# One decoder layer on one core: the router finishes its expert weights later, gathers spread over more banks, and the first norm's factor is computed ahead of the parameters

## The chip, the cores and the metric

The kernel is one launch on one core of a Trainium2 chip. The metric is the device time of that launch in microseconds (us), lower is better. The engines are PE (TensorE), DVE (VectorE), ACT (ScalarE), POOL (GpSimd) and SP (SyncE, which here only issues DMAs). They run side by side and meet at semaphores. A bank is one of the eight PSUM banks into which PE writes.

## The reference, cut to what matters

One layer for 256 tokens of width 2048, in float32: a norm and one big projection, two mixers (sparse attention and RWKV-7), an output projection, attention over 256 memory tokens, and then the part that the change is mostly about, a mixture of experts in two levels. A token picks the best of 4 groups, and inside it the best 2 of 8 experts:

```python
def hier_moe(h, wg_r, bg_r, we_r, be_r, w_gate, w_up, w_down):
    hf = h.reshape(B * T, D)
    p_group = jax.nn.softmax((hf @ wg_r + bg_r).astype(jnp.float32), axis=-1)
    pg_top, g_idx = lax.top_k(p_group, 1)
    e_logits = (hf @ we_r + be_r).reshape(n, N_GROUPS, EXPERTS_PER_GROUP)
    e_logits = jnp.take_along_axis(e_logits, g_idx[:, :, None], axis=1)[:, 0]
    p_exp = jax.nn.softmax(e_logits.astype(jnp.float32), axis=-1)
    pe_top, e_idx = lax.top_k(p_exp, TOP_K_INNER)
    wts = pg_top * pe_top / jnp.sum(pe_top, axis=-1, keepdims=True)
    ...
    for grp in range(N_GROUPS):
        sl = slice(grp * EXPERTS_PER_GROUP, (grp + 1) * EXPERTS_PER_GROUP)
        hid = (jax.nn.silu(jnp.einsum("nd,edf->nef", hf, w_gate[sl]))
               * jnp.einsum("nd,edf->nef", hf, w_up[sl]))
        y = y + jnp.einsum("nef,efd->nd", hid * combine[:, sl, None], w_down[sl])
```

The first norm, `h = rmsnorm(x, ln1_g)`, is the other place that the change touches.

## The kernel before, in words

**Precision.** Matmuls that need float32 accuracy are done in three passes: an operand is split into a high part (ACT writes a copy) and a low part (DVE subtracts that copy from the value), and PE multiplies hi by hi, hi by lo and lo by hi.

**Start.** SP loads x and a table of small parameters. ACT sums the squares of x. DVE waits first for PE's transposed parameter table (`prm`, lines 1835 to 1839), copies it, and then computes the norm's factor and two diagonal matrices (`diagonals("n1", D)`, helper lines 1804 to 1817). PE transposes x through these diagonals (line 784), and DVE multiplies each result by the gain (line 1823).

**Router.** PE computes 36 logits per token (line 1195) and turns them (line 1206). DVE then works through a chain of tiny instructions, each waiting for the one before it through a semaphore (`link`): the one-hot of the group `goh`, the logits of the chosen group `d8`, the best and second expert `o1`, `o2` (helper `first_only`, three instructions), their weights `w1_`, `w2_`, and the table `comb` of weights by expert. ACT gives two exponentials on the way, `ge` and `e2`. With the mark `routed` PE counts each token's place in its group (`pos`, lines 1210 to 1212) and the size of each group (`cnt`, line 1215). DVE makes from these the one-hot matrices `G` of two groups of up to 128 tokens each (line 2218) and the flag `oflag` of a group over 128 (line 2223, mark `most`). This input has no such group, so the extra pass over one isn't run.

**Gather.** `gather(k)` on PE first computes each slot's weights from `comb` (line 1228, bank 0, eight matmul records; DVE copies them to `wcol`, line 2241), and then in eight steps f the gathered activations of two groups (line 1238), step f into bank 3 or 2. For each step ACT writes the high part (line 1681) and DVE the low part (line 2246), after which the bank is free. The first gather opens the expert stage, the second comes 15 experts later, at group 2.

**Experts.** An expert is six half units of weights of 2048 columns each: four for gate and up (offsets 0 to 3), two for down (4, 5). SP loads them (line 689, 694), ACT splits off the high part (line 1696), DVE the low part (line 2156), PE multiplies (line 1275 gate and up, line 1294 down). There are three split buffers, so a half unit can be split when PE has read the third one before it. Between gate/up and down stand ACT's tanh (line 1709), DVE's two products `hid` (`hidden_values`, lines 2259 to 2263), and a transpose (line 1283). The kernel runs one expert's gate and up ahead of its down. Between two groups of eight experts PE scatters the sums back to tokens (line 1259), and DVE adds them to x (line 2236).

**Order.** Each engine executes its own list, written out by hand, strictly in order. Before the loop over experts DVE's list is: router chain, low part of half unit 0, gather, low parts of half units 1 to 3, eleven instructions on overflow (`posm`'s and `comb`'s extra column, then the visit count, mark `ovi`), the read of that count into a register, and `hidden_values(0)`.

Of the kernel before, what the change touches and what calls it, by code (L numbers as in the profile page):

```python
# [23 lines left out]
ALU = mybir.AluOpType  # L24
# [49 lines left out]
def decoder_layer(nc, x_in, mem, ln1_g, w_in, cmp_pos_k, cmp_w1_k, cmp_w2_k, cmp_pos_v, cmp_w1_v,  # L74
# [5 lines left out]
    with ctx:  # L80
# [411 lines left out]
        dve_r = Progress(sem("dve_router"), ["h3lo", "gd", "m2", "routed", "posm", "most", "ovi"])  # L492
# [25 lines left out]
        SRC_NA, SRC_N2, SRC_MEM = 1, 5, 13  # L518

# [220 lines left out]
        def _(pe):  # L740
# [468 lines left out]
            pe.wait_ge(*dve_r.at("routed"))  # L1209
# [9 lines left out]

            def gather(k):  # L1220

                pe.wait_ge(onehot_g, k + 1)
                if k:
                    pe.wait_ge(dve_sc, 8 * (2 * k - 1))
                for g in range(2 if k < NGR // 2 else 1):
                    at = (2 * k + g) * EPG
                    for tt in range(NT):
                        mm = pe.matmul(bank[0][:, g * EPG:g * EPG + EPG], G[:, tt, g * P:g * P + P].bitcast(F32),
                                       comb[:, tt, at:at + EPG], start=tt == 0, stop=tt == 1)
                mm.then_inc(pe_cm, 1)  # L1230
                for f in range(8):
                    if f >= 2:
                        pe.wait_ge(dve_hs, 8 * k + f - 1)
                    for j in range(2):
                        c = 2 * f + j
                        for tt in range(NT):
                            for part in range(2):
                                mm = pe.matmul(bank[3 - f % 2][:, j * 2 * P:j * 2 * P + 2 * P],
                                               h3[part][:, tt, c * P:c * P + P],
                                               G[:, tt, :], start=tt + part == 0, stop=tt + part == 2)  # L1240
# [115 lines left out]
        def _(act):  # L1356
# [319 lines left out]
            def gathered(k):  # L1676
                for f in range(8):
                    act.wait_ge(pe_hs, 8 * k + f + 1)
                    for j in range(2):
                        c = 2 * f + j  # L1680
                        ins = A(hs[0][:, :, c, :], b2(3 - f % 2)[:, j, :].rearrange("p (g s) -> p g s", g=2), ACT.Copy,
# [22 lines left out]
            act.wait_ge(*dve_r.at("m2"))  # L1704
            A(e2, m2, ACT.Exp).then_inc(*act_r.mark("e2"))
# [60 lines left out]
            nov = act.value_load(count_i[0:1, 0:1], min_val=0, max_val=1)  # L1766
            tanh(0, 0, 4)
# [29 lines left out]
        def _(dve):  # L1797
# [36 lines left out]

            dve.wait_ge(*pe_c.at("prm"))
# [5 lines left out]
            diagonals("n1", D)  # L1841
# [345 lines left out]
            first_only(o1, eq8, wtie)  # L2187
            link(V.scalar_tensor_tensor(out=flat(d8), in0=flat(o1), scalar=BIG, in1=flat(d8), op0=ALU.mult, op1=ALU.add))
            V.tensor_reduce(m2, d8, AX.X, ALU.max).then_inc(*dve_r.mark("m2"))
            dve.wait_ge(*act_r.at("e2"))  # L2190
            link(TT(eq8, d8, bc(m2.unsqueeze(2), 2, EPG), ALU.is_equal))
            first_only(o2, eq8, wtie)
            link(V.tensor_scalar(w1_, e2, 1.0, None, ALU.add))
            link(V.reciprocal(w1_, w1_))
            link(TT(w1_, w1_, pg, ALU.mult))
            link(TT(w2_, w1_, e2, ALU.mult))
            link(V.tensor_scalar(w1_, w1_, 0.5, None, ALU.mult))
            link(V.tensor_scalar(w2_, w2_, 0.5, None, ALU.mult))
            link(TT(c8, o1, bc(w1_.unsqueeze(2), 2, EPG), ALU.mult))
            link(TT(eq8, o2, bc(w2_.unsqueeze(2), 2, EPG), ALU.mult))  # L2200
            link(TT(c8, c8, eq8, ALU.add))
            link(TT(o1, o1, o2, ALU.add))
            for t in range(NT):
                g4 = bc(goh[:, t].unsqueeze(2), NGR, EPG)
                ins = TT(comb[:, t, 0:NE].rearrange("p (g j) -> p g j", g=NGR), g4, bc(c8[:, t].unsqueeze(1), NGR, EPG),
                         ALU.mult)
            ins.then_inc(*dve_r.mark("routed"))
            dve.wait_ge(*dve_r.at("routed"))
# [7 lines left out]
            for tt in range(NT):  # L2216
# [3 lines left out]


            dve.wait_ge(*pe_r.at("cnt"))
            V.tensor_scalar(oflag, bank[2][:, 128:128 + NGR], float(CAP), None, ALU.is_gt)\
                .then_inc(*dve_r.mark("most"))
            weights(None, 0)
# [12 lines left out]
            def gathered(k):  # L2238
                dve.wait_ge(pe_cm, k + 1)
                w = 2 * EPG if k < NGR // 2 else EPG  # L2240
                V.tensor_copy(wcol[:, 0:w], bank[0][:, 0:w])
                for f in range(8):
                    dve.wait_ge(act_hs, 8 * k + f + 1)
                    for j in range(2):
                        c = 2 * f + j
                        ins = V.scalar_tensor_tensor(out=hs[1][:, :, c, :],
                                                     in0=b2(3 - f % 2)[:, j, :].rearrange("p (g s) -> p g s", g=2),
# [31 lines left out]
            def first_body(n):  # L2279
# [22 lines left out]
                if n:  # L2302
                    add(n - 1, 6)
                    add(n - 1, 7)
                onehots(n, 0)
# [18 lines left out]
            dve.wait_ge(*dve_r.at("most"))  # L2324
            link(TT(geq, pg_, bc(oflag.unsqueeze(1), 2, NGR), ALU.mult))
            link(V.tensor_reduce(rtop, geq, AX.X, ALU.add))
# [186 lines left out]
```

## Time and profile before

| what | us |
|---|---|
| three runs | 1781.06, 1775.94, 1781.58 (median 1781.06) |
| profiled execution, its own time | 1781.15 |
| its span | 1779.4 |
| busy: PE, DVE, ACT, POOL | 1691.9, 1011.4, 760.7, 71.5 |
| mean granted clock of PE | 0.983 of full speed |

The span is what the trace covers, some 1.75 us less than the execution's own time. A busy share near 95% of PE doesn't say that PE bounds every stage. For that the chain of work that ended last is to be read, stage by stage: it names at each moment the instruction that the end was waiting for. Bracketed times in the timeline are idle time of an engine ahead of an instruction, with what released it.

### The profile page before, as it was taken

What the parts mean: (1) busy time and instruction counts of PE and PEld (TensorE: products, weight loads), DVE (VectorE), ACT (ScalarE), POOL (GpSimd) and SP (SyncE); (2) the same over time, 40 slices, a digit from 0 to 9 for tenths busy, and PEclk for the clock granted to TensorE, in tenths of its full rate; (3) what the DMA queues carried; (4) which work ended last, traced back from release to release, by engine and by line L of the source; (5) the groups of instructions that cost most, each with busy time, mean ns of one, the idle gap of its engine ahead of it and who ended that gap; (6) DMA issues with size and microseconds to landing.
All of it is one profiled execution on the core that took longest, in us unless ns stands there. A gap on an engine that the chain in (4) does not pass through costs nothing.

```text
span 1779.4 us, 29542 instructions
## 1 busy us (share of the span) xinstructions
PE 1691.9 (95%) x12488; PEld 1471.4 (83%) x12488; DVE 1011.4 (57%) x1261; ACT 760.7 (43%) x964; POOL 71.5 (4%) x136
## 2 busy tenths in 40 slices
PE   6999999999999999999999999969999999999996
PEld 5887887878878989999999989857887887888784
DVE  1142533424435544445453334468889888889986
ACT  1011210111115444444443334426776766777674
POOL 4001010101100000000000000000000000000000
PEclk9899999999999999999999999989999999999999
DMA  7420613306126434446545235229998996999993
GB/s 209 142 95 3 196 49 127 117 2 196 49 97 211 147 125 136 143 143 198 180 142 189 94 104 187 95 101 358 375 378 329 378 373 239 369 374 361 347 374 153
DMA packets 173745, 350.77 MB, mean 197 GB/s; under 512 B 12915, under 2 KB 145612, under 8 KB 148172
## 3 DMA queue, kind: packets, MB, share of 16 engines
q1 hardware_dynamic: 173644, 349.30, 55.6%
q8 instruction: 78, 1.28, 0.3%
q14 instruction: 23, 0.19, 0.0%
HBM read 347.18 MB, written 2.10 MB: 196 GB/s over the span
## 4 chain that ended last, share of the span: by engine, by line
PE 86%; DVE 10%; ACT 2%; POOL 1%; issue 1%; SPq 0%; DMA 0%; DVEq 0%; ACTq 0%
PE bank L1275 18%; PE bank L765 16%; PE bank L1127 10%; PE bank L1294 9%; PE bank L1131 5%; PE bank L1023 4%; PE bank L1030 4%; DVE split L2156 2%; PE bank L784 2%; PE bank L754 2%; PE bank L870 1%; DVE piece L1977 1%; PE bank L885 1%; PE bank L880 1%; DVE arena_phases L2236 1%; PE bank L1177 1%
## 5 line engine op out<-in xcount | busy, mean ns | idle before, releaser
L2156 DVE TENSOR_TENSOR split<-weights_raw,split 128x2048 fp32r<-128x2048 f32 x192 | 438.6, 2290 | 55.9 <-ACT split L1696 53.2
L1696 ACT CAST split<-weights_raw 128x2048 fp32r<-128x2048 f32 x192 | 367.1, 1913 | 94.0 <-PE bank L1275 48.0
L1275 PE MATMUL bank<-split,gathered_hi 128*128 128x512 f32 x1024 | 321.3, 395 | 7.4 <-DVE split L2156 7.4
L765 PE MATMUL bank<-arena_fixed 128*128 128x256 f32 x1280 | 302.1, 388 | 0.0
L765 PEld LDWEIGHTS bank<-arena_fixed 128*128 128x128 f32 x1280 | 238.1, 191 | 42.7 <-issue 9.1
L1275 PEld LDWEIGHTS bank<-split,gathered_hi 128*128 128x128 f32 x1024 | 190.9, 189 | 48.3 <-DVE split L2156 9.6
L1275 PE MATMUL bank<-split,gathered_lo 128*128 128x512 f32 x512 | 201.0, 393 | 0.0
L1127 PE MATMUL bank<-loop_split,act_over_concat 128*128 128x256 f32 x768 | 164.8, 283 | 0.0
L1294 PE MATMUL bank<-split,hidden_hi 128*128 128x512 f32 x512 | 161.0, 395 | 1.5 <-DVE hidden_lo L2268 1.0
L2060 DVE TENSOR_TENSOR loop_split<-arena_fixed,loop_split 128x2048 fp32r<-128x2048 f32 x48 | 107.8, 2288 | 90.7 <-ACT loop_split L1593 90.7
L1127 PEld LDWEIGHTS bank<-loop_split,act_over_concat 128*128 128x128 f32 x768 | 129.1, 192 | 0.1
L1127 PE MATMUL bank<-loop_split,act_over_hT 128*128 128x256 f32 x512 | 119.0, 283 | 0.0
L1294 PEld LDWEIGHTS bank<-split,hidden_hi 128*128 128x128 f32 x512 | 95.8, 187 | 25.3 <-issue 1.2
L1275 PEld LDWEIGHTS bank<-split,gathered_lo 128*128 128x128 f32 x512 | 96.8, 189 | 21.0
L1294 PE MATMUL bank<-split,hidden_lo 128*128 128x512 f32 x256 | 100.9, 394 | 0.0
L1977 DVE TENSOR_TENSOR piece<-arena_fixed,piece 128x1024 fp32r<-128x1024 f32 x60 | 72.5, 1220 | 41.4 <-ACT piece L1429 41.2
L1131 PE MATMUL bank<-act_over_concat,loop_split 128*128 128x256 f32 x512 | 92.3, 283 | 0.0
L1593 ACT CAST loop_split<-arena_fixed 128x2048 fp32r<-128x2048 f32 x48 | 89.2, 1917 | 5.1 <-PE bank L1023 3.1
L1127 PEld LDWEIGHTS bank<-loop_split,act_over_hT 128*128 128x128 f32 x512 | 89.1, 192 | 0.2 <-DVE loop_split L2060 0.2
L1429 ACT CAST piece<-arena_fixed 128x1024 fp32r<-128x1024 f32 x60 | 62.3, 1044 | 53.2 <-PE bank L1030 25.7
L1131 PEld LDWEIGHTS bank<-act_over_concat,loop_split 128*128 128x128 f32 x512 | 79.9, 192 | 0.0
L1030 PE MATMUL bank<-mem_lo,piece 128*128 128x256 f32 x256 | 73.1, 286 | 0.0
(394 smaller groups left out, 2395.8 us busy)
## 6 DMA issues: line engine op xcount, KB each, us to landing
weights_raw<-in_moe_w_gate_dram SPq DMA_DIRECT2D x64, 1024.0 KB, 4.9
weights_raw<-in_moe_w_up_dram SPq DMA_DIRECT2D x64, 1024.0 KB, 7.0
weights_raw<-in_moe_w_down_dram SPq DMA_DIRECT2D x32, 2048.0 KB, 7.7
arena_fixed<-in_w_in_dram SPq DMA_DIRECT2D x22, 2048.0 KB, 8.8
arena_fixed<-in_wv_mem_dram SPq DMA_DIRECT2D x8, 2048.0 KB, 8.7
arena_fixed<-in_w_out_dram SPq DMA_DIRECT2D x8, 2048.0 KB, 8.2
arena_fixed<-in_wq_mem_dram SPq DMA_DIRECT2D x8, 2048.0 KB, 8.2
arena_fixed<-in_wo_mem_dram SPq DMA_DIRECT2D x8, 2048.0 KB, 8.2
```

The costliest lines, as they stand in the source:

```text
L765: mm = pe.matmul(b[:, half * T:half * T + T], w[:, c, half * P:half * P + P], hT[:, c, :], start=st, stop=en)
L1023: mm = pe.matmul(b[:, half * UC:half * UC + UC], mem_x(x_, c)[:, half * P:half * P + P], pieces[p % NPB][:, w_, at:at + UC], start=False, ...
L1030: mm = pe.matmul(b[:, half * T:half * T + T], pieces[p % NPB][:, w_, at:at + P], mem_x(x_, c), start=c + t == 0, stop=c == NC - 1 and t == 2)
L1127: mm = pe.matmul(b, src(x_, cc)[:, half * P:half * P + P], lspl[2 * s + h][:, y_, c * UC:c * UC + UC], **flags)
L1131: mm = pe.matmul(b, lspl[2 * s + h][:, y_, at:at + P], src(x_, cc), **flags)
L1275: mm = pe.matmul(bank[parity][:, :], hs[a][:, group % 2, NC // 4 * off + c, :], sl[:, b, c * 2 * FF:(c + 1) * 2 * FF], start=off + c + k == 0,
L1294: mm = pe.matmul(bank[4 + q][:, :], tTs[a][:, f, :], sl[:, b, q * 512:q * 512 + 512], start=start and f + k == 0, stop=stop and f + k == 3)
L1593: nc.scalar.copy(lspl[2 * s + h][:, 0, :], slot(s)[:, at:at + HU]).then_inc(loop_hi, 1)
L1696: nc.scalar.copy(split_half(i, 0, j), raw_half(j, hf, tail)).then_inc(act_hi, 1)
L1977: V.tensor_tensor(piece_half(p, 1), raw_piece(p), piece_half(p, 0).bitcast(F32), ALU.subtract) .then_inc(piece_lo, 1)
L2060: V.tensor_tensor(sl[:, 1, :], slot(s)[:, r:r + HU], sl[:, 0, :].bitcast(F32), ALU.subtract)\
L2156: V.tensor_tensor(split_half(i, 1, j), raw_half(j, hf, tail), split_half(i, 0, j).bitcast(F32), ALU.subtract).then_inc(dve_lo, 1)
```

## The change

There are three edits.

1. At the start `diagonals("n1", D)` stands ahead of DVE's wait for the parameter table.
2. The router: DVE forms `goh` first, without the sum and reciprocal of the group softmax, and marks it; PE's `pos` and `cnt` wait for this mark instead of `routed`. DVE goes on to the chosen logits up to `eq8`, then makes positions, `G`, `oflag` and the visit count (`ovi`). The rest of the chain is a function `expert_weights()`, called behind the low parts of half units 1 to 3. One addition (`o1` plus `o2`, whose sum nothing reads) is gone. The slot weights of the first gather are a function of their own, called on PE behind the fourth half unit, into bank 4. The overflow column (`overflow_slots`) is computed in the first expert's body, and DVE reads the visit count after the first group of experts. PE reads it behind the first half unit.
3. The first gather uses banks 3, 2, 4, 5, 6, 7 in turn, later ones 3, 2, 0. The first multiplication after a later gather waits for the sixth low part.

```diff
-            pe.wait_ge(*dve_r.at("routed"))
+            pe.wait_ge(*dve_r.at("goh"))
             pe.matmul(bank[3][:, 0:NGR], strictU, goh[:, 0, :], start=True, stop=True)
...
+        def gather_banks(k):
+            return (3, 2, 0) if k else (3, 2, 4, 5, 6, 7)
...
+            def gather(k):
+                pe.wait_ge(onehot_g, k + 1)
+                banks = gather_banks(k)
+                if k:
+                    pe.wait_ge(dve_sc, 8 * (2 * k - 1))
+                    slot_weights(k, 0)
                 for f in range(8):
-                    if f >= 2:
-                        pe.wait_ge(dve_hs, 8 * k + f - 1)
+                    if f >= len(banks):
+                        pe.wait_ge(dve_hs, 8 * k + f - len(banks) + 1)
+                    elif banks[f] == 0:
+                        pe.wait_ge(dve_hs, 8 * k + 1)
...
-                    pe.wait_ge(dve_hs, 8 * (group // 2) + 2 * off + 2)
+                    pe.wait_ge(dve_hs, 8 * (group // 2) + max(2 * off + 2, 6 if group else 0))
...
             pe.wait_ge(*dve_r.at("most"))
-            pe.wait_ge(*dve_r.at("h3lo"))
             gather(0)
-            for off in range(4):
-                gate_up(None, off, 0, 0, fresh=True)
+            gate_up(None, 0, 0, 0, fresh=True)
             pe.wait_ge(*dve_r.at("ovi"))
             nov = pe.value_load(count_i[0:1, 0:1], min_val=0, max_val=1)
+            for off in range(1, 4):
+                gate_up(None, off, 0, 0, fresh=True)
+            pe.wait_ge(*dve_r.at("routed"))
+            slot_weights(0, 4)
...
+            dve.wait_ge(*pool_c.at("ident"))
+            diagonals("n1", D)
             dve.wait_ge(*pe_c.at("prm"))
             link(V.tensor_copy(prm, bank[2][:, 0:2 * P]))
...
-            diagonals("n1", D)
...
-            dve.wait_ge(*act_r.at("ge"))
-            link(V.tensor_reduce(pg, ge, AX.X, ALU.add))
-            link(V.reciprocal(pg, pg))
+            dve.wait_ge(*dve_r.at("gd"))
             link(V.tensor_scalar(geq, gd_, 0.0, None, ALU.is_equal))
-            first_only(goh, geq, wtie[:, 0:NGR])
+            link(TT(goh, geq, bc(wtie[:, 0:NGR].unsqueeze(1), 2, NGR), ALU.mult))
+            link(V.tensor_reduce(rtop, goh, AX.X, ALU.max))
+            TT(goh, goh, bc(rtop.unsqueeze(2), 2, NGR), ALU.is_equal).then_inc(*dve_r.mark("goh"))
...
-            link(TT(o1, o1, o2, ALU.add))
...
             gathered(0)
             for off in range(1, 4):
                 weights(None, off)
+            expert_weights()
+            slot_weights(0, 4)
             hidden_values(0, 0, 0)
             for n in range(NGR):
                 group(n)
+                if n == 0:
+                    dve.wait_ge(*dve_r.at("ovi"))
+                    nov = dve.value_load(count_i[0:1, 0:1], min_val=0, max_val=1)
```

DVE's list between the group counts and the first split, before. `arena_phases` holds all small router values, `split0` to `split2` the split buffers, `gathered_lo` the low part of the gathered tokens.

```order
L2199 TENSOR_TENSOR arena_phases<-arena_phases 128x16
L2200 TENSOR_TENSOR arena_phases<-arena_phases 128x16
L2201 TENSOR_TENSOR arena_phases<-arena_phases 128x16
L2202 TENSOR_TENSOR arena_phases<-arena_phases 128x16
L2205 TENSOR_TENSOR arena_phases<-arena_phases 128x32 x2
L2211 SCALAR_TENSOR_TENSOR arena_phases<-bank3,arena_phases 128x2x4
L2213 TENSOR_SCALAR arena_phases<-arena_phases 128x2x4
L2214 COPY arena_phases<-arena_phases 128x2
L2218 TENSOR_SCALAR gather_onehots_76<-arena_phases 128x128 x4
L2223 TENSOR_SCALAR arena_phases<-bank2 128x4
L2156 TENSOR_TENSOR split0_64<-weights_raw_67,split0_64 128x2x4x256
L2241 COPY arena_phases<-bank0 128x16
```

And after, at the same place:

```order
L2202 TENSOR_TENSOR arena_phases<-arena_phases 128x16
L2203 TENSOR_SCALAR arena_phases<-arena_phases 128x16
L2207 SCALAR_TENSOR_TENSOR arena_phases<-bank3,arena_phases 128x2x4
L2209 TENSOR_SCALAR arena_phases<-arena_phases 128x2x4
L2210 COPY arena_phases<-arena_phases 128x2
L2214 TENSOR_SCALAR gather_onehots_76<-arena_phases 128x128 x4
L2217 TENSOR_SCALAR arena_phases<-bank2 128x4
L2220 TENSOR_TENSOR arena_phases<-arena_phases 128x4
L2221 TENSOR_REDUCE arena_phases<-arena_phases 128x1
L2222 TENSOR_REDUCE arena_phases<-arena_phases 128x1
L2223 SCALAR_TENSOR_TENSOR arena_phases<-arena_phases 128x1
L2225 TENSOR_SCALAR arena_phases<-arena_phases 128x1
```

The weights' arithmetic no longer stands ahead of the positions (line 2207, which reads bank 3), and the visit count follows line 2217.

DVE's list behind the low part of the fourth half unit, before. `visit_counts` is the table that the engines read into registers.

```order
L2156 TENSOR_TENSOR split0_64<-weights_raw_67,split0_64 128x2x4x256
L2325 TENSOR_TENSOR arena_phases<-arena_phases 128x8
L2326 TENSOR_REDUCE arena_phases<-arena_phases 128x2
...
L2336 TENSOR_SCALAR arena_phases<-arena_phases 128x1
L2337 CAST visit_counts<-arena_phases 128x3
L2339 TENSOR_LOAD visit_counts
L2339 ISA x2
L2259 COPY arena_phases<-arena_phases 128x1
```

And after:

```order
L2172 TENSOR_TENSOR split0_64<-weights_raw_67,split0_64 128x2x4x256
L2183 TENSOR_TENSOR arena_phases<-arena_phases 128x16
L2184 TENSOR_REDUCE arena_phases<-arena_phases 128x2
L2185 TENSOR_TENSOR arena_phases<-arena_phases 128x16
...
L2247 TENSOR_TENSOR arena_phases<-arena_phases 128x16
L2248 TENSOR_TENSOR arena_phases<-arena_phases 128x16
L2251 TENSOR_TENSOR arena_phases<-arena_phases 128x32 x2
L2281 COPY arena_phases<-bank4 128x16
L2305 COPY arena_phases<-arena_phases 128x1
```

Where 11 instructions and a register read stood between the split and the copy of line 2259, there are now 22 instructions and a copy out of bank 4, for which PE has to multiply in between.

PE's list around the start of the gather, before. The matmuls on `arena_phases` alone are `pos` and `cnt`.

```order
L1206 MATMUL bank3<-arena_fixed,arena_phases 128x36 x2
L1210 MATMUL bank3<-arena_phases 128x4
L1211 MATMUL bank3<-arena_phases 128x4
L1212 MATMUL bank3<-arena_phases 128x4
L1215 MATMUL bank2<-arena_phases 128x4 x2
L1228 MATMUL bank0<-arena_phases,gather_onehots_76 128x8 x4
L1238 MATMUL bank3<-gather_onehots_76,h3_hi_68 128x256
```

And after:

```order
L1212 MATMUL bank3<-arena_fixed,arena_phases 128x36 x2
L1216 MATMUL bank3<-arena_phases 128x4
L1217 MATMUL bank3<-arena_phases 128x4
L1218 MATMUL bank3<-arena_phases 128x4
L1221 MATMUL bank2<-arena_phases 128x4 x2
L1251 MATMUL bank3<-gather_onehots_76,h3_hi_68 128x256
```

The slot weights are no longer between the counts and the gather.

## Rows read from the trace of the kernel before

**Rows 1.** Timeline of the start: start us, length us, engine, line, instruction, count, [idle before].
```profile
10.04 0.19 ACT L1406 ACTIVATION_READ_ACCUMULATOR arena_fixed<-arena_fixed 128x1 f32 x1
...
11.82 0.42 PE L792 MATMUL bank<-arena_fixed,arena_phases 128*128 128x128 f32 x1
...
13.12 0.18 DVE L1808 TENSOR_SCALAR arena_fixed<-arena_fixed 128x2 f32<-128x2 f32 x1
...
13.77 0.68 DVE L1816 TENSOR_SCALAR norm_diagonals<-arena_fixed 128x128 f32<-128x128 f32 x2
...
14.50 10.04 PE L784 MATMUL bank<-norm_diagonals,arena_fixed 128*128 128x128 f32 x64 [2.27 <-DVE norm_diagonals L1816]
```

**Rows 2.** Timeline of the router.
```profile
1158.43 0.37 ACT L1701 COPY arena_phases<-bank 36x256 f32<-36x256 f32 x1 [4.45 <-PE bank L1195]
...
1159.73 0.17 DVE L2174 TENSOR_TENSOR arena_phases<-arena_phases 128x8 f32<-128x8 f32 x1
...
1160.57 0.17 DVE L2178 TENSOR_SCALAR arena_phases<-arena_phases 128x8 f32<-128x8 f32 x1
...
1161.38 0.26 DVE L2182 TENSOR_TENSOR arena_phases<-arena_phases 128x64 f32<-128x64 f32 x1
...
1162.34 0.17 DVE L2186 TENSOR_SCALAR arena_phases<-arena_phases 128x16 f32<-128x16 f32 x1
...
1166.70 0.29 DVE L2205 TENSOR_TENSOR arena_phases<-arena_phases 128x32 f32<-128x32 f32 x2
...
1168.60 0.17 DVE L2211 SCALAR_TENSOR_TENSOR arena_phases<-bank,arena_phases 128x8 f32<-128x8 f32 x1 [1.61 <-PE bank L1212]
...
1170.00 0.15 DVE L2223 TENSOR_SCALAR arena_phases<-bank 128x4 f32<-128x4 f32 x1
```

**Rows 3.** Chain that ended last, first gather to first expert: start us, length us, what.
```profile
1170.23 1.86 PE bank L1228 x8
1172.09 1.92 PE bank L1238 x8
1174.03 0.85 ACT gathered_hi L1681 x2
...
1185.77 0.88 DVE gathered_lo L2246 x2
...
1188.90 8.51 PE bank L1275 x36
...
1201.98 8.52 PE bank L1275 x24
```

**Rows 4.** Timeline of DVE behind the first gather.
```profile
1193.16 0.16 DVE L2325 TENSOR_TENSOR arena_phases<-arena_phases 128x8 f32<-128x8 f32 x1
...
1194.31 0.17 DVE L2331 TENSOR_TENSOR arena_phases<-arena_phases 128x4 f32<-128x4 f32 x1
...
1197.85 0.15 DVE L2259 COPY arena_phases<-arena_phases 128x1 f32<-128x1 f32 x1 [2.40 <-ACT arena_phases L1709]
...
1198.36 0.48 DVE L2263 SCALAR_TENSOR_TENSOR arena_phases<-arena_phases,bank 128x256 f32<-128x256 f32 x1
```

**Rows 5.** Stretches: from:to, length, busy us of PE PEld DVE ACT POOL, clock, DMA share, GB/s.
```profile
1160.00:1163.00 3.00, 0.00 (x0) 0.00 (x0) 2.38 (x14) 0.14 (x1) 0.00 (x0) 1.00 0.00 0
1163.00:1167.00 4.00, 0.00 (x0) 0.00 (x0) 3.18 (x19) 0.20 (x1) 0.00 (x0) 0.56 0.00 0
```

**Rows 6.** Chain that ended last, second gather.
```profile
1461.83 0.79 PE bank L1228 x8
1462.62 1.05 PE bank L1238 x8
...
1473.76 5.49 PE bank L1275 x24
```

**Rows 7.** Timeline of DVE, first expert's end.
```profile
1219.14 4.49 DVE L2156 TENSOR_TENSOR split<-weights_raw,split 128x2048 fp32r<-128x2048 f32 x2
```

**Rows 8.** Chain that ended last, same time.
```profile
1222.03 5.44 PE bank L1275 x24
```

**Rows 9.** Waits of ACT for a DMA, expert stage: total us, times, longest.
```profile
ACT split L1696 <- DMA weights_raw<-in_moe_w_up_dram: 0.7, 1, 0.7
```

More of the change, by code:

```diff
@@ L1237, in gather @@
                             for part in range(2):
-                                mm = pe.matmul(bank[3 - f % 2][:, j * 2 * P:j * 2 * P + 2 * P],
+                                mm = pe.matmul(bank[banks[f % len(banks)]][:, j * 2 * P:j * 2 * P + 2 * P],
                                                h3[part][:, tt, c * P:c * P + P],
@@ L2224, in _ @@
                 .then_inc(*dve_r.mark("most"))
+            dve.wait_ge(*dve_r.at("most"))
+            link(TT(otmp4, oflag, kval, ALU.mult))
+            link(V.tensor_reduce(osum[:, 0:1], oflag, AX.X, ALU.add))
+            link(V.tensor_reduce(osum[:, 1:2], otmp4, AX.X, ALU.add))
+            link(V.scalar_tensor_tensor(out=osum[:, 2:3], in0=osum[:, 0:1], scalar=-(NGR - 1.0), in1=osum[:, 1:2],
+                                        op0=ALU.mult, op1=ALU.add))
+            link(V.tensor_scalar(osum[:, 2:3], osum[:, 2:3], NGR - 1.0, None, ALU.add))
@@ new lines, in _, with expert_weights @@
+            V.tensor_copy(count_i[:, 0:3], osum).then_inc(*dve_r.mark("ovi"))
+            def expert_weights():
+                first_only(o1, eq8, wtie)
+                link(V.scalar_tensor_tensor(out=flat(d8), in0=flat(o1), scalar=BIG, in1=flat(d8), op0=ALU.mult, op1=ALU.add))
+                V.tensor_reduce(m2, d8, AX.X, ALU.max).then_inc(*dve_r.mark("m2"))
+                dve.wait_ge(*act_r.at("ge"))
+                link(V.tensor_reduce(pg, ge, AX.X, ALU.add))
+                link(V.reciprocal(pg, pg))
+                dve.wait_ge(*dve_r.at("m2"))
+                link(TT(eq8, d8, bc(m2.unsqueeze(2), 2, EPG), ALU.is_equal))
+                first_only(o2, eq8, wtie)
+                dve.wait_ge(*act_r.at("e2"))
+                link(V.tensor_scalar(w1_, e2, 1.0, None, ALU.add))
+                link(V.reciprocal(w1_, w1_))
+                link(TT(w1_, w1_, pg, ALU.mult))
+                link(TT(w2_, w1_, e2, ALU.mult))
+                link(V.tensor_scalar(w1_, w1_, 0.5, None, ALU.mult))
+                link(V.tensor_scalar(w2_, w2_, 0.5, None, ALU.mult))
+                link(TT(c8, o1, bc(w1_.unsqueeze(2), 2, EPG), ALU.mult))
+                link(TT(eq8, o2, bc(w2_.unsqueeze(2), 2, EPG), ALU.mult))
+                link(TT(c8, c8, eq8, ALU.add))
+                for t in range(NT):
+                    g4 = bc(goh[:, t].unsqueeze(2), NGR, EPG)
+                    ins = TT(comb[:, t, 0:NE].rearrange("p (g j) -> p g j", g=NGR), g4, bc(c8[:, t].unsqueeze(1), NGR, EPG),
+                             ALU.mult)
+                ins.then_inc(*dve_r.mark("routed"))
+                dve.wait_ge(*dve_r.at("routed"))
@@ new lines, in overflow_slots @@
+            def overflow_slots():
+                link(TT(geq, pg_, bc(oflag.unsqueeze(1), 2, NGR), ALU.mult))
+                link(V.tensor_reduce(rtop, geq, AX.X, ALU.add))
+                link(V.tensor_scalar(posm[:, :, NGR:].rearrange("p t o -> p (t o)"), rtop, -float(CAP), None, ALU.add))
+                o4 = bc(oflag.unsqueeze(1).unsqueeze(1), 2, EPG, NGR)
+                link(TT(tmp, comb[:, :, 0:NE].rearrange("p t (g j) -> p t j g", g=NGR), o4, ALU.mult))
+                V.tensor_reduce(comb[:, :, NE:], tmp, AX.X, ALU.add).then_inc(*dve_r.mark("spare"))
@@ L2304, in first_body @@
                     add(n - 1, 7)
+                else:
+                    overflow_slots()
                 onehots(n, 0)
```

68 lines of the change are left out of this document (18 added, 50 removed).

## The prediction, made before the changed kernel was run

> **What bounds the kernel now.** The chain that ended last was read first, then the waits, then the timeline around the two places that the change touches. On that chain PE has most of the span, and between stages it hands over to small DVE and ACT work. Three such places matter.
>
> At the start PE's transposes of x begin at 14.50, released by DVE's diagonals (13.77 to 14.45), although ACT had the sum of squares at 10.23 [rows 1]. PE's transposed parameters ended at 12.24, and DVE had waited for them before it began on the norm at 13.12 [rows 1].
>
> In the router DVE works alone: from the group's maximum at 1159.73 to the last weights at 1166.99, and to `oflag`, which ends at 1170.15 [rows 2]. The reader is to see instructions of 0.17 us that start 0.2 us apart: what costs is their number. PE's clock was granted in full until 1163 and is at a mean of 0.56 from then to 1167, PE idle throughout [rows 5]; so part of the first gather ran at 1.2 GHz: its first step of eight matmuls took 1.92 us, the first step of the second gather 1.05 [rows 3, 6].
>
> From 1188.90 PE runs dense, stops near 1197.4, and starts on the first expert at 1201.98 [rows 3]; from there it is the chain, with weights arriving in time (ACT waited once for a DMA, 0.7 us [rows 9]). So what makes PE start earlier should move the end by as much.
>
> **Start.** The diagonals took 13.12 to 14.45, so 1.33 us [rows 1]. Now they begin at 10.27 and end near 11.6, before PE's parameters at 12.24. PE goes on at once at 12.3 in place of 14.50: 2.2 us won. Were the diagonals slowed to double length, 12.9 would be the start, 1.6 won. DVE's copy of the table hides behind PE's first transposes. Bounds: 0, if a weight load becomes what the projection waits for, and 2.3.
>
> **Router up to the gather.** Dropped ahead of `goh` are two instructions and the wait for ACT: 1160.57 becomes 1159.94, 0.63 us. From 1160.57 to 1161.38 the four instructions up to `goh` stay, 0.81: `goh` is there at 1160.75. The five to `eq8` (1161.38 to 1162.51, with handover 1.17) end at 1161.9 [rows 2]. PE's `pos` took from 1166.99 to 1168.60, 1.6 us, at the low clock; at the full one, which rows 5 show for that time, about half of it. DVE needs 1.15 us for the five, so it waits for nothing, or 0.4 us. From 1168.60 to 1170.15 stays: 1.55. So `most` comes at 1163.5 to 1163.9; I take 1163.6, that is 6.5 us earlier. The slot weights, 1.86 us ahead of the gather, go [rows 3]. The gather starts at 1163.65 in place of 1172.09, 8.4 us earlier.
>
> **First gather.** Before, step f waited for the low part of step f-2: from 1172.09 to 1186.65, 14.56 us for PE, ACT 0.85, DVE 0.88 in turn [rows 3]. With six banks nothing waits but the last two steps, and for work long done. DVE first does six instructions for the count (1.15, as the six from 1194.31 on [rows 4]) and half unit 0 (2.25, half of 4.49 [rows 7]), until 1167.0, then needs eight times 0.9. That is its floor, 1174.2. PE at the low clock needs about 1.75 a step (1.92 with the drain at its end), at the full 1.05. Four slow and four fast steps, 7.0 and 4.2, then ACT and DVE, 1.73: the last low part at 1176.6, in place of 1186.65. Won at this point: 10.05. Bounds: 7.3 (all eight slow) and 12.4 (DVE's floor).
>
> On this the Trainium skill (TensorE: Matmul & The Clock Gate, "What's actually happening") says that the throttled state is the default and that activity releases it, at a point that varies from run to run. By the rule the clock could fall where it fell before, or not, the tiny matmuls of `pos` counting for little; the trace agrees as far as the fall at 1163 goes, 4.6 us after PE's logits, its last dense work, ended near 1158.4 [rows 2, 5]. By the rule's better case the sum is 1.7 us lower, a rival below.
>
> **Behind the gather.** Low parts 1 to 3 keep their places. Let S be the end of the last, 1193.16 before [rows 4]; PE ended half unit 3 at S+4.2 (1188.90 and 8.51) and started the first expert at S+8.8 [rows 3]. What lies there now: 22 instructions. From 1161.38 to 1166.99 is 5.61; less the five that stay in front, 1.17, less the dropped addition, 0.2, plus sum and reciprocal, 0.4: 4.6 at most, with the wait for ACT in it [rows 2]. Then PE's slot weights (0.79 at the full clock [rows 6], 1.86 at the low) and the copy 0.2: S+5.7. `hidden_values` 1.0 (1197.85 to 1198.84 [rows 4]), the low part 2.3: PE starts at S+9.0. ACT is no longer in the way: its tanh waits for S+4.2 and its high part ends near S+6.6. So the expert weights' 4.6 us hide behind PE's three half units, and 0.2 us is lost. Bounds: 0 and 1.3 lost.
>
> PE's first 24 matmuls after that idle time took 8.52, where the same 24 later take 5.44 [rows 3, 8]: 3.1 us for the low clock. Now the idle stretch is cut by eight small matmuls into 0.4 and 3.1 us. I count half, 1.5 won; bounds 0 and 3.1.
>
> **First experts.** `overflow_slots` (five instructions, 1.15, 1193.16 to 1194.31 [rows 4]) now stands ahead of the split at 1219.14, whose first half ends at 1221.4, while PE needs it at 1222.03 [rows 7, 8]: 0.6 is covered, 0.55 lost. DVE's read of the visit count stood in idle time: it fitted into 2.4 us [rows 4]. Now it stands between two splits with 0.6 us of cover. Between 0 and 1.8 lost; I take 0.3, as it is a single register. The Trainium skill (Runtime: NRT & Kernel Launch, "Instruction fetch mechanics") gives about 200 ns a register for such loads, which would be nothing lost; no row here shows it. Queued behind it is only the next split, for which PE waits.
>
> **Second gather.** Before, 1461.83 to 1473.76, of which 1.84 are slot weights and first step [rows 6]. With three banks step 2 still waits for the first low part (1462.62 + 1.05 + 0.85 + 0.88 = 1465.4), then PE runs six steps without a stop, 6.3: 1471.8, 2.0 won. The new wait for the sixth low part ends near 1471.4, so it costs nothing; bounds 0.5 and 2.7 won.
>
> **Sum.** 2.2 + 10.05 + 2.0 + 1.5 - 0.2 - 0.55 - 0.3 = 14.7. The profiled execution took 1781.15, so 1766.4; the median of the runs is 1781.06, the same.
>
> **Rivals.** (a) The clock stays up in the gather and behind the prologue: 1.7 and 1.6 more, 1763.1. For it: from the logits' end at 1158.4 to the next work of PE it is 2.3 us, and 5.3 to the gather, where it was 8.6 to the first small matmul [rows 2]. Against: N=4 matmuls are little work. Chance 0.3.
>
> (b) Gains don't carry through: the earlier start meets weights that aren't there, or DVE, now late at the first expert, holds PE for some experts. Of DVE's slack, 0.6 us an expert, a backlog of 2 us would last three experts, and the start's 2.2 could go: 1781.15 - 14.7 + 2.2 + 3.7 = 1772.1. Against: one DMA wait of 0.7 us in the whole stage [rows 9]. Chance 0.13.
>
> (c) The change doesn't do what it says: positions early but ACT or the first load decides when the experts start; only start and second gather remain, 4.2 us: 1777.0. Nothing in the rows speaks for it, since SP's loads are released by DVE's splits, which move along. Chance 0.04.
>
> (d) Slower: the clock. If PE, restarted from broken work, stays at 1.2 GHz through the gather and the first experts, each 24 matmuls cost 3.1 us more [rows 3, 8], some 9 an expert of three such blocks. Two experts so cost 18, more than the 14.7 won: 1784.6. It decides from five such blocks on. Against: before, the clock came back within the first 24. Chance 0.03.
>
> **Chances.** Forecast 0.5, (a) 0.3, (b) 0.13, (c) 0.04, (d) 0.03. About 0.3%, 5.3 us, is what a measurement of this kernel can tell from no change; the three runs shown lie 5.6 apart. Faster takes in the forecast, (a) and nearly all of (b): 0.91; same 0.06; slower 0.03. The range reaches from (a) with the better bound of the gathers, 1759.5, to (b), 1772.5.
>
> **What would show it.** PE's first transposes at 12.3; `cnt` right behind the logits' transposes; last low part of the first gather some 12 us earlier than before on the span's axis, with start and gather together; PE's first expert 12 earlier; the second gather about 10 us from slot weights to first multiplication in place of 11.9; a PE wait for the split in the second expert below 1 us. The prediction is wrong if DVE, not PE, is on the chain for more than those two experts, or if PE's projection at the start waits for a DMA.

## The result, and the profile after

The changed kernel took 1765.58 us (median of 5 runs, 1765.19 to 1766.41); the kernel before took 1781.58 on the same chip (5 runs, 1775.94 to 1784.14). The ratio is 0.991, with a 95% interval of 0.9896 to 0.9924. The profiled execution took 1765.84 us, its span is 1764.1 against 1779.4 before. The forecast was 1766.4. Beside the repeated runs below, one of the 11 executions of the kernel before took 3510 us; the ratios there leave it out as slow.

The start first. Chain that ended last, changed kernel (start us, length us, what):

```profile
12.24 8.60 PE bank L790 x64
...
21.60 7.17 PE bank L763 x32
...
49.76 4.26 PE bank L769 x32
54.02 6.83 PE bank L780 x32
```

The same chain, kernel before:

```profile
25.33 7.17 PE bank L757 x32
...
53.49 3.68 PE bank L763 x32
57.17 6.32 PE bank L774 x32
```

The transposes of x start at 12.24 where they started at 14.50 [rows 1], the forecast 12.3. The projection behind them starts at 21.60; before it was 25.33, so 3.7 us were ahead there. The reader is to see the last two rows of each: the matmuls of lines 769 and 780 are narrow (24 columns), took 3.68 and 6.32 before, and take 4.26 and 6.83 now. The stretches (from:to, length, busy us of PE, of PEld, the weight loads, of DVE, ACT and POOL with counts, granted clock, DMA share, GB/s) say why. The last one is of the kernel before:

```profile
49.00:53.00 4.00, 4.00 (x33) 3.48 (x31) 0.00 (x0) 0.00 (x0) 0.00 (x0) 0.96 0.28 86
53.00:57.00 4.00, 4.00 (x20) 4.00 (x21) 0.00 (x0) 0.00 (x0) 0.00 (x0) 0.50 0.00 0
57.00:61.00 4.00, 4.00 (x20) 4.00 (x20) 0.00 (x0) 0.12 (x1) 0.00 (x0) 0.50 0.00 0
```
```profile
53.00:57.00 4.00, 4.00 (x35) 3.59 (x34) 0.00 (x0) 0.00 (x0) 0.00 (x0) 1.00 0.22 68
```

PE is busy without a pause there, and the granted clock is at 0.50, 1.2 GHz, from 53; the kernel before had 1.00 in 53 to 57 and fell at 57.6. The clock costs time again at the second norm, whose transposes start 3.07 us earlier (903.26 against 906.33). Chain there, after and before:

```profile
903.26 10.34 PE bank L790 x64
```
```profile
906.33 9.04 PE bank L784 x64
```

The clock was 0.50 from the first of these transposes on until 909.4; in the kernel before it fell only at 907.8 and was back at 911. At the logits' transposes, 1157.27 against 1158.84, 1.57 us of the start's gain are left.

The router. Timeline (start us, length us, engine, line, instruction, count, [idle before]):

```profile
1156.85 0.37 ACT L1716 COPY arena_phases<-bank 36x256 f32<-36x256 f32 x1 [4.53 <-PE bank L1201]
...
1160.34 0.17 DVE L2207 SCALAR_TENSOR_TENSOR arena_phases<-bank,arena_phases 128x8 f32<-128x8 f32 x1
...
1161.74 0.16 DVE L2217 TENSOR_SCALAR arena_phases<-bank 128x4 f32<-128x4 f32 x1
```

From ACT's copy to the overflow flag's instruction it was 11.57 us [rows 2] and is 4.89, so 6.7 less; DVE's first instruction on the positions (line 2207) no longer waits for PE, where it stood 1.61 before [rows 2]. Then the gather, the chain again:

```profile
1160.95 0.88 DVE gather_onehots L2214 x4
...
1161.97 9.44 PE bank L1251 x64
1171.44 0.85 ACT gathered_hi L1696 x2
...
1173.19 6.61 DVE split L2172 x3
...
1184.04 1.07 PE bank L1231 x8
...
1186.41 2.21 DVE split L2172
...
1188.66 7.39 PE bank L1288 x24
```

The eight steps, with a handover to ACT and DVE at each of them before, are now one piece of 9.44 us on PE. The last low part ends at 1173.19 instead of 1186.65 [rows 3], 13.46 earlier, 11.9 of them since the logits. The reader is to see in the last rows what stands between the splits and PE's restart: the slot weights, which the gather no longer waits for, 4.6 us ahead of PE's restart. Stretches of the same time:

```profile
1158.00:1161.00 3.00, 1.28 (x10) 1.19 (x10) 2.52 (x15) 0.21 (x1) 0.00 (x0) 1.00 0.00 0
1161.00:1164.00 3.00, 2.03 (x9) 2.05 (x10) 2.79 (x12) 0.00 (x0) 0.00 (x0) 0.67 0.00 0
1164.00:1167.00 3.00, 3.00 (x22) 3.00 (x21) 2.49 (x5) 2.04 (x5) 0.00 (x0) 0.76 0.02 5
1167.00:1170.00 3.00, 3.00 (x27) 3.00 (x26) 2.74 (x8) 2.64 (x8) 0.00 (x0) 1.00 0.00 0
```

The clock is in full at 1158 to 1161 and falls at 1162.0, just after the gather began; at 1165.4 it is back. Before, it fell at 1163 with PE long idle [rows 5], and the gather's first steps ran at the low level.

The second expert's start (chain), and the DVE instruction behind the register read (timeline):

```profile
1208.08 5.74 PE bank L1288 x24
```

```profile
1306.37 6.83 DVE L2172 TENSOR_TENSOR split<-weights_raw,split 128x2048 fp32r<-128x2048 f32 x3 [0.64 <-issue]
```

And the second gather, chain:

```profile
1448.34 0.79 PE bank L1231 x8
1449.13 1.06 PE bank L1251 x8
...
1452.01 6.16 PE bank L1251 x48
...
1458.21 5.69 PE bank L1288 x24
```

Before it was 11.93 us from slot weights to first multiplication, with a handover at each step [rows 6]; now 9.87, one handover and then 48 matmuls in one piece.

### The profile page after: what moved, and what is told of

Same layout as the page of the kernel before. It is cut to its first block, busy times and chain, and to the rows that moved or that the text cites. A ratio compares the mean times of both kernels' runs of the same rounds, so it can differ in the third digit from the quotient of the medians.

```text
span 1764.1 us, 29546 instructions
## 1 busy us (share of the span) xinstructions
PE 1687.6 (96%) x12488; PEld 1468.0 (83%) x12488; DVE 1011.5 (57%) x1260; ACT 760.9 (43%) x964; POOL 71.6 (4%) x136
## 4 chain that ended last, share of the span: by engine, by line
PE 85%; DVE 10%; ACT 2%; POOL 1%; issue 1%; DMA 1%; SPq 0%; DVEq 0%; ACTq 0%
PE bank L1288 17%; PE bank L771 16%; PE bank L1133 10%; PE bank L1307 9%; PE bank L1137 5%; PE bank L1029 4%; PE bank L1036 3%; DVE split L2172 3%; PE bank L790 2%; PE bank L760 2%; DVE piece L1993 1%; PE bank L876 1%; PE bank L891 1%; PE bank L886 1%; DVE arena_phases L2276 1%; PE bank L1183 1%
## 5 line engine op out<-in xcount | busy, mean ns | idle before, releaser
L1137 PE MATMUL bank<-act_over_hT,loop_split 128*128 128x256 f32 x256 | 72.4, 283 | 0.0
```

The lines of the kernel that those rows point to most:

```text
L1137: mm = pe.matmul(b, lspl[2 * s + h][:, y_, at:at + P], src(x_, cc), **flags)
```

## Experiments

In the kernels of this section, L is the start of the logits' transposes in the profile. Steps behind it are counted from L, as L itself differs by 1 to 2 us between kernels whose instructions are the same up to there. The kernel before has the last low part of the first gather at L+27.81 and the first expert at L+43.14; the changed kernel at L+15.92 and L+31.39. Ratios are to the kernel before, executed on the same chip beside each run; runs of different batches are compared by them and by their profiles, of which there is one for each run.

**Start alone** (the kernel before, with the diagonals ahead of the wait for PE's parameters).

```diff
+            dve.wait_ge(*pool_c.at("ident"))
+            diagonals("n1", D)
             dve.wait_ge(*pe_c.at("prm"))
             ... copy of the table ...
-            diagonals("n1", D)
```

> The kernel before with one edit: the first norm's factor and diagonals ahead of the wait for the parameters. Theory (the start's gain carries to the end, less what PE's clock takes back): PE's transposes of x at 12.3 in place of 14.50, the projection's first matmul near 21.6 in place of 25.33, and of these 3.7 us only 1 to 2 are left at the end: 1779 to 1780.5, a ratio of 0.999. Rival 1 (gain carries in full): 1777.4. Rival 2 (it is all given back before the router): 1781.

Measured: 1781.57 us against 1783.36, ratio 0.9989 (0.9976 to 1.0002). Transposes at 12.2, projection at 21.86, 3.5 earlier; at L 0.9 is left. The clock is at 0.53 in 53 to 57 already, and the second norm's transposes take 10.13 us. Alone, the edit can't be told from nothing, nor from the rival by which all 3.7 us carry to the end (1777.4, a ratio of 0.998).

**Banks alone** (the kernel before with six and three banks in the gathers).

```diff
+        def gather_banks(k):
+            return (3, 2, 0) if k else (3, 2, 4, 5, 6, 7)
...
-                    if f >= 2:
-                        pe.wait_ge(dve_hs, 8 * k + f - 1)
+                    if f >= len(banks):
+                        pe.wait_ge(dve_hs, 8 * k + f - len(banks) + 1)
```

> The kernel before with one edit: six banks for the first gather, three for the second, router as it was. Theory (the gather was bound by the handover of two banks): first gather's last low part 3.0 us earlier, second gather 2.0 us shorter, in sum 1776.1. Rival (DVE is the bound in the gather, so banks give little in the first): only the second's 2.0, 1779.1.

Measured: 1775.75 us, ratio 0.9953 (0.9934 to 0.9972). The profiled executions differ by 4.8 us, where 5.0 were expected; the medians differ by 7.6, more than the profile accounts for. Last low part at L+25.08, 2.7 earlier; the slot weights and the gather, from its chain:

```profile
1170.18 1.85 PE bank L1234 x8
1172.03 10.06 PE bank L1247 x64
```

The gather's 64 matmuls in one piece, 10.06 us, though the clock was at 0.50 until 1177.2; the handovers made 12.8 from the same start to the last ACT copy. The second gather is 9.1 us from its first step to the multiplication, before 11.1 (1462.62 to 1473.76 [rows 6]).

**Router alone** (the changed kernel, with the start as before and two banks in both gathers).

```diff
-            return (3, 2, 0) if k else (3, 2, 4, 5, 6, 7)
+            return (3, 2)
```

> The changed kernel with the start as before and two banks in every gather: the router's edit alone. Theory (three separate gains that add): 15.3 less 1.6 and 5.0, so 8.7 us won, 1772.4. Rival (banks and router overlap, since the early gather runs at another clock): 1770 or 1775, with the difference to be seen in the number of gather steps at 1.2 GHz.

Measured: 1774.69 us, ratio 0.9949 (0.9929 to 0.9969). Won were 8.7 us by the medians, as expected. Last low part at L+19.30, 8.5 earlier, first expert at L+34.77, 8.4 earlier. With the banks' 2.8 that makes 11.1 at the first expert; together they have 11.75. The three ratios multiplied give 0.9891, their combination was measured at 0.991: no loss by the combination that the intervals would show.

**Expert weights at once** (the changed kernel, with the expert weights ahead of the first low part of the splits, and ACT's second exponential, which they need, ahead of its splits too; banks and positions as changed).

```diff
+            expert_weights()
             weights(None, 0)
...
-            expert_weights()
             slot_weights(0, 4)
```

> The changed kernel with one thing undone: the expert weights are computed before the first split's low part, where DVE is early, and no longer behind the fourth half unit. Theory (DVE is now the bound from the gather to the first expert, and its 22 small instructions, 4.4 us, cost about the same wherever they stand on that path): gather's last low part 3.6 us later, PE's first expert 3.4 us later, 1769.0. Rival (the deferral hides them fully, so undoing it costs all 4.4 us): 1770.0. Rival (DVE had slack during the gather, PE being its bound): under 2 us, 1767.

Measured: 1770.36 us, ratio 0.9927 (0.9908 to 0.9946). Last low part at L+18.57, first expert at L+35.47, so 4.1 us are lost by standing in front, where the instructions take 4.2 (1179.79 to 1183.99 in the changed kernel's chain). That the two are nearly alike is chance: the last low part is only 2.65 late, and 1.4 more are lost behind it, where the weights no longer stand. By the times alone the two kernels aren't told apart (0.9908 to 0.9946 against 0.9896 to 0.9924); the profile tells them apart. Its timeline shows both ends of it, PE at its half units and DVE at the copy of the slot weights:

```profile
1178.80 0.73 PE L1288 MATMUL bank<-split,gathered_hi 128*128 128x512 f32 x2 [2.79 <-DVE split L2172]
...
1180.74 1.05 PE L1288 MATMUL bank<-split,gathered_hi 128*128 128x512 f32 x2
...
1183.25 0.62 PE L1288 MATMUL bank<-split,gathered_hi 128*128 128x512 f32 x2
```
```profile
1189.70 0.17 DVE L2282 COPY arena_phases<-bank 128x16 f32<-128x16 f32 x1 [6.55 <-PE bank L1231]
```

A pair of matmuls goes from 0.73 to 1.05 and back to 0.62 us: PE stopped 2.79 us for the splits, its clock was at 0.50 from 1179.8 to 1183.1, and its three half units end late. DVE then stands 6.55 us waiting for PE's slot weights, in time which the changed kernel fills with the expert weights and waits 1.2.

**Overflow column behind the expert weights** (from the second expert's split to the place where DVE waits 1.2 us for PE's slot weights).

```diff
-                else:
-                    overflow_slots()
...
             expert_weights()
+            overflow_slots()
             slot_weights(0, 4)
```

> The changed kernel with the overflow column moved: computed directly behind the expert weights, where DVE waits 1.22 us for PE's slot weights, and no longer in the first expert's body. Theory (its 1.15 us cost PE 0.5 us at the second expert, because the split there had 0.6 us of cover): the second expert's first matmul follows the first expert's last with no wait, 0.5 us won, the first expert starts at the same distance from the logits; below what five rounds resolve, so it is read from the trace. Rival: the wait for PE is not idle time for DVE and the first expert starts 1.1 us later.

Measured: 1765.47 us, ratio 0.9907 (0.9889 to 0.9926), span 1766.0. By time it is level with the changed kernel (0.991). First expert at L+31.24, not later, so the 1.15 us did fit into the wait. Its chain shows the second expert's first matmuls without their wait:

```profile
1209.65 5.44 PE bank L1288 x24
```

It starts at L+50.46, in the changed kernel at L+50.81: 0.35 won there, 0.63 by the second gather, since these 24 matmuls take 5.44 in place of 5.74. Its L is 1159.19, 1.9 later than the changed kernel's, and hides that in the span.

**First half unit before the gather** (the last, and half unit 1 ahead of the gather's low parts).

```diff
+            weights(None, 1)
             gathered(0)
-            for off in range(1, 4):
+            for off in range(2, 4):
                 weights(None, off)
```

> As the last, and the low part of half unit 1 computed ahead of the gather's low parts. Theory (DVE bounds the way from the gather to the first expert, and only the idle moments at the gather's start, some 0.9 us, can be filled): first expert 0.9 us earlier as seen from the logits, 1.4 us won in all, 1764.2; the load of the next expert's first half is issued 8 us earlier and ACT's wait for a DMA, 0.94 us, goes. Rival (the gather's low parts, now 2.2 us later, delay PE): no gain or a loss of 1.

Measured: 1764.36 us, ratio 0.9896 (0.9874 to 0.9917). First expert at L+29.86, 1.5 earlier than the changed kernel's and 1.4 than the last one's, where 0.9 was expected; at the second gather it is 1.4 ahead of the changed kernel, as expected, and ACT's wait for a DMA is gone. But its chain has, behind an idle time of PE of the same length (3.50 us, in the changed kernel 3.57):

```profile
1188.14 8.35 PE bank L1288 x24
```

8.35 against 7.39, 7.66 and 7.69 in the changed kernel, its second execution (below) and the last experiment's kernel: the clock was at 0.50 already when PE restarted, and was back at 1193.7 only. Whether by the edit or by chance one profile can't tell. The second expert starts at L+49.71, 1.1 ahead.

**Two half units of the next expert before the expert weights** (the last, and so that PE has 24 more matmuls while DVE works on the expert weights; ACT's splits and PE's slot weights are moved along with them, which the cut doesn't show).

```diff
+            weights(0, 0)
+            weights(0, 1)
             expert_weights()
             overflow_slots()
```

> As the last, and the first two half units of the second expert (her gate and up are multiplied before the first expert's down) are split on ACT and DVE before tanh and before the expert weights; PE's slot weights stand behind these two. Theory (PE's idle 4 to 5 us ahead of the first expert comes from the order on ACT and DVE, tanh and weights ahead of splits, and not from missing data): PE goes from the fourth half unit to the next without a stop and later waits once, for the load of the second half; its fifth half unit behind the gather's starts 4 us earlier than in the changed kernel, 1761. Rival (the loads bound it): 1764, with ACT waiting for a DMA in place of PE waiting for DVE.

Measured: 1764.75 us, ratio 0.99 (0.9881 to 0.9919), span 1763.0. The second expert starts at L+48.23, 2.6 ahead, the second gather 2.7 ahead; the restart's 24 matmuls take 7.36. The expectation of 1761 was missed. Of its theory one half came out: PE runs without a stop from the gather to the end of the sixth half unit, at 1188.5. But behind it PE waits for DVE in three places (0.35, 1.30 and 1.54 us) until 1193.46, so its idle time was moved rather than taken away. The time is that of the rival (1764), the loads as its cause are not shown: ACT waited for a DMA 0.8 us there, and PE for DVE as before.

**A later start** (the changed kernel with six instructions of DVE ahead of the norm's factor, to delay the transposes).

```diff
             dve.wait_ge(*pool_c.at("ident"))
+            dve.wait_ge(*act_n.at(("n1", "sq")))
+            for _ in range(6):
+                link(V.tensor_scalar(dg[:, 0, :], ident, 1.0, None, ALU.mult))
             diagonals("n1", D)
```

> The changed kernel with six extra instructions of DVE, on the diagonals' buffer, ahead of the norm's factor: PE's transposes start 1.3 us later, at 13.5. Theory (of the start's gain the clock takes a share that depends on where its changes fall, so the end does not follow the start one to one): projection's first matmul anywhere from 22 to 24, and the logits' transposes within 1 us of the changed kernel's, 1765 to 1767, not resolved from it. Rival (each us at the start is a us at the end): 1767 in all and 1.3 us later at the logits.

Measured: 1767.16 us, ratio 0.992 (0.9903 to 0.9938), span 1765.8. Its chain and one stretch:

```profile
14.14 10.13 PE bank L790 x64
...
25.05 7.17 PE bank L763 x32
...
53.20 3.68 PE bank L769 x32
56.88 6.24 PE bank L780 x32
```
```profile
53.00:57.00 4.00, 4.00 (x36) 3.87 (x35) 0.00 (x0) 0.00 (x0) 0.00 (x0) 1.00 0.18 55
```

The transposes are 1.9 us late (1.3 was meant), the projection 3.45, L only 1.34. The narrow matmuls take 9.92 where they took 11.09, the second norm's transposes 9.04 in place of 10.34: the kernel is slow where the kernel before was slow, and fast where it was fast. The expectation was missed in its places (projection from 22 to 24, L within 1 us), and the numbers of the rival came out (1767, L 1.3 late). Against the changed kernel's second profile, which follows, the 1.8 us at the transposes are 1.84 at L. So this run doesn't show that the clock takes a share of a delay at the start; the two comparisons differ by 0.5 us, and that is what one execution or another makes.

**The changed kernel once more, and the last version beside it** (both unaltered).

> The changed kernel once more, unaltered, to see what of a profile's times is the kernel's own. If the place at which the clock falls at the start belongs to the kernel, the logits' transposes start at 1157.3 us again, within 0.3, and the clock is 0.50 from 53 us on. If it belongs to the single execution, they start anywhere between 1157 and 1159 us, the range that kernels with the same code up to there have shown (1157.27 to 1159.19), and the steps behind them keep their distance: last low parts 15.9 us behind, first expert 31.4 us behind, within 0.2. Time about 1765.5 us.

> The kernel with the overflow column moved, the first weight half unit split before the gather and two half units of the next expert before the expert weights, unaltered, beside the changed kernel on one chip. Counted from the logits' transposes its second expert starts 2.6 us earlier than the changed kernel's (48.2 against 50.8 us) and its second gather 2.7 us earlier. If the lateness of the transposes in its first profile (1158.17 against 1157.27 us) belongs to that execution, its time is 2 to 2.7 us under the changed kernel's, a ratio between the two of 0.9985 to 0.9989; if it belongs to the kernel, 1 us under.

Measured: the changed kernel 1766.53 us (1763.83 to 1769.26, 6 runs), ratio to before 0.9914 (0.9897 to 0.9931). Its L is 1156.77, 0.5 from the first profile's and just outside both ranges of the expectation; what decides is that the clock wasn't at 0.50 from 53 on. Last low part L+15.82, first expert L+31.30, within the 0.2 expected. The clock fell later in the same code:

```profile
53.00:57.00 4.00, 4.00 (x32) 4.00 (x31) 0.00 (x0) 0.00 (x0) 0.00 (x0) 0.82 0.00 0
```

against 0.50 in the first profile. This execution has its projection at 23.23 only, 2.1 ahead of the kernel before; its narrow matmuls take 9.96 and the second norm's transposes 9.04, as before, and at L it is 2.07 ahead. So the same kernel once wins at the first transposes and pays back more behind, and once does neither. Where the clock falls belongs to the execution: it fell at 52.7 in the first and at 55.5 in the second, 2.9 and 4.1 us behind the first narrow matmul. The Trainium skill (TensorE: Matmul & The Clock Gate, "What's actually happening") says of the point at which the clock rises that it varies from run to run; the trace shows the same of its fall.

The last version took 1764.63 us (1761.98 to 1767.59, 6 runs), ratio to before 0.9905 (0.9887 to 0.9922). Its median is 1.9 under the changed kernel's, with ranges that overlap; its span is 1.8 under (1762.8 to 1764.6), its second gather 3.0 earlier counted from L. L came out at 1158.31, at 1158.17 the first time; the changed kernel's two are 1157.27 and 1156.77. That about 1 us came back with the kernel, though the instructions up to L are the same; with two profiles of each it can be chance. Why is open. It isn't shown by time that this version beats the changed one: what speaks for it is the profile alone.

## Why the prediction was right, and which terms were not

The gain between the profiled executions was 15.3 us, the sum had 14.7. The mechanism was right in each place that it named, and its terms were off both ways: the gather gave 1.8 more, start, restart and overflow column together 1.25 less. That the total lies within 0.6 is in part this cancelling, so luck. Its steps:

- **Start, 2.2.** Right at the place it named (12.24). The transposes then gave 1.5 more (8.60 against 10.06): PE went from some 7 matmuls a microsecond to 11 or 12 at 15 instead of at 20. The granted clock has 1.00 in all these stretches, so that this is the clock is argued, not shown; in the second execution the transposes took 10.09, and the 1.5 was luck. 1.1 went back in the narrow matmuls, 1.3 in the second norm. 1.57 was left at the router, in the second execution 2.07, with the start alone 0.9. That the clock adds and takes on the way stood in neither sum nor rivals. All profiles together bound the term poorly: the eight with the start's edit and no delay have L from 1156.77 to 1159.19, 1158.0 on average, the three without it 1158.79, 1158.84 and 1160.62, so 1.4 on average with a scatter as large. The 2.2 are shown at the transposes; what of them reaches the end is not measured better than that.
- **Router and gather, 10.05.** Measured 11.9, from L. The router came out as forecast: 6.7 for 6.5. The gather was sized with four slow steps; the clock was low for about the first two, 1162.0 to 1165.4, so 9.44 us in place of 11.2. These 1.8 are all that rival (a) gave for the gather (1.7), though the clock did fall: for a clock that stays up the prediction's own floor of DVE, 12.4 won, makes it 2.35. So rival (a) didn't come true, its price was too low. The single edits give 8.5 for router and 2.7 for banks.
- **Expert weights hidden, 0.2 lost.** PE starts the first expert at S+8.86, S being the end of the last low part (1179.8); forecast S+9.0, before S+8.8. That they are hidden is shown by the kernel that takes them out of there: 4.1 lost. They took 4.2, not 4.6.
- **Clock at the restart, 1.5.** Measured 1.13 (8.52 to 7.39), 0.86 in the second execution (7.66). Other kernels with 3.5 to 3.8 us of idle time there show 7.32 to 8.35. The idle stretch was 3.57; the prediction's own times (S+9.0 less S+4.6 and 0.8) make 3.6 of it too, not the 3.1 that it has.
- **Overflow column, 0.55 lost.** Measured 0.5 in the wait and 0.3 in the 24 matmuls behind it (5.74 against 5.44); the run that moved it got 0.63 back.
- **Register read, 0.3 lost.** DVE's gap before the split is 0.64 where other splits follow at 0.21, so the read cost 0.43; PE lost 0.16 (5.60 against 5.44), the rest was cover. The trace has the load of the register itself at 555 ns, and at 552 in the kernel before, where the prediction could have looked it up. The Trainium skill's figure (Runtime: NRT & Kernel Launch, "Instruction fetch mechanics") is about 200 ns a register; the trace disagrees, and the measurement decides.
- **Second gather, 2.0.** Measured 2.06. The new wait of PE for the sixth low part cost about 0.2, not nothing: that low part ended near 1458.1, PE began at 1458.21, and the 24 matmuls take 5.69 in place of 5.49. The kernels with this wait all show 5.69 to 5.73, router alone, which has two banks and not this wait, 5.45.

On the span's axis: 1.57 + 11.75 at the first expert (the gather's 11.9 less 0.15 behind it), + 1.13 - 0.8 - 0.16 + 2.06 = 15.55; the end has 15.3. Of the 0.25 between them 0.2 are the 24 matmuls behind the second gather (5.69 against 5.49).

Some sums of the prediction don't come out of its own terms. Rival (b) adds up to 1772.35, not 1772.1, and its 3.7 has no row. Two experts of three blocks at 3.1 each make 18.6 in (d), so 1785. The best bound of every term together gives 1760.7, so the range's lower end, 1759.5, lies 1.2 beyond them. None of this moves the forecast.

Rival (b), gains that don't carry, named DVE and weights. Behind the restart DVE held PE longer than before only in the second expert (0.51) and at the register read, and ACT waited for a DMA twice in the expert stage, 1.9 us in all, against once, 0.7, before; PE's gain didn't shrink by it. (c) fell, as the first expert came 11.75 earlier counted from L. (d) fell: the clock came back within the first 24 matmuls.

## What to carry to other kernels

A chain of many tiny instructions on one engine should be cut at the first value that the next stage needs, and the rest put where that engine waits for another: here 4.2 us of instructions cost next to nothing behind PE's half units and 4.1 in front of them. When a stage hands over between three engines at every step, the number of output buffers can set its time: banks that stood idle in this stage took 2.7 us off the first gather and 2.1 off the second. Steps in two profiles are compared from a common event near them, not from the span's start: the clock moves the axis by 1 to 2 us.

## What the runs showed of the hardware that was not expected

PE, busy 4.00 of 4.00 us in matmuls of 24 columns, is granted 1.2 GHz in every kernel here from some point between 52.7 and 57.6 us on, 2.9 to 4.3 us behind the first of these matmuls, and again in the transposes of the second norm near 905, behind a pause of 3 us. The 64 transposes there take either 9.04 us (the kernel before, banks alone, late start, the changed kernel's second execution) or 10.1 to 10.3 (all others), the narrow matmuls 9.8 to 10.0 or 10.2 to 11.1; the four profiles with 9.04 are the four with 9.8 to 10.0. What decides between the two was not found. The start of the logits' transposes, L, so lay between 1156.77 and 1160.62 us, where the start's edit alone would make 2.3 of it; the latest was the kernel with router alone, whose instructions up to L are those of the kernel before (1158.84).
